# Mixture-of-experts layer of a diffusion trunk: one pass for each expert, ordered by row count, with extra rows beside the two largest and 64 rows in float32 for the smallest

## The chip, the cores and the metric

The kernel runs on one core of one Trainium2 chip. The metric is the device time of one execution in microseconds (us), as the median of repeated runs. The core has a matmul engine (TensorE, in the profile PE, and PEld for its weight loads), three engines for elementwise work (VectorE or DVE, ScalarE or ACT, GpSimd or POOL) and a queue of transfers that SyncE (SP) issues. They run side by side and wait for each other by semaphores.

## The reference

Two layers work on 384 tokens (128 of a prompt, 256 latents) of width 1024, all in float32. The change touches the last sub-layer, a mixture of eight experts of which each token takes two:

```python
D_MODEL, N_EXPERTS, TOP_K, D_FF_EXPERT = 1024, 8, 2, 1792

def swiglu(h, wg, wu, wd):
    return (jax.nn.silu(h @ wg) * (h @ wu)) @ wd

def moe_swiglu(h, w_router, wg, wu, wd):
    logits = (h @ w_router).astype(jnp.float32)
    top_v, top_i = lax.top_k(logits, TOP_K)
    top_w = jax.nn.softmax(top_v, axis=-1)
    gates = jnp.einsum('blk,blke->ble', top_w, jax.nn.one_hot(top_i, N_EXPERTS))
    y = jnp.zeros_like(h)
    for e in range(N_EXPERTS):
        y = y + gates[..., e:e + 1] * swiglu(h, wg[e], wu[e], wd[e])
    return y
```

An expert's three matrices are 1024x1792, 1024x1792 and 1792x1024 float32, 22.0 MB together. Evaluating the reference's router on its own inputs (seed 0) gives these tokens for experts 0 to 7: 60, 86, 80, 54, 96, 175, 136, 81. They sum to 768, two for each of the 384 tokens. Before this sub-layer come an even layer (convolution and pooling mixer, dense SwiGLU) and the odd layer's attention; after it a layer norm.

## The kernel before

Up to the router nothing is touched. There the kernel counts each expert's tokens on the chip and numbers them. The work of the experts is cut into **items**: an item is up to 128 rows of one expert. An expert with more than 128 rows gets a second item, and its weights are loaded a second time. The table of items (`ranks` and `items_of`, L1519 to L1536) is computed by VectorE in the middle of the first item; `more_items` gives the count of items after the first, and each engine runs one loop over them.

An item has 30 **pieces**. Each of its two halves of 896 hidden columns has eight gate/up pieces (128 input rows by 896 gate and 896 up columns, 896 KB) and seven down pieces (128 hidden rows by 1024 columns, 512 KB). SP loads each piece into one of six slots `ERAW` (L500 to L515). ScalarE casts it to fp32r, which is the high part (`expert_high`, L975), and VectorE subtracts that from the piece, which leaves the low part (`expert_low`, L1482). Both parts go to one of six slots `EWS`. The raw slot is free again when VectorE is done with it (`e_lo`), the split slot when TensorE is (`e_used`).

TensorE makes each product of the split numbers by three matmuls (`product`, L1854 to L1860): high by high, high by low, low by high. The rows of the item, 128 tokens, are the stationary side, so every matmul has 128 output rows whether they hold tokens or not. `gate_up` (L2144) has four column quarters of 448 for each piece, `down` (L2157) two halves of 512.

The loop body on TensorE is: gate/up of the first half, the down products of the second half of the item before, `turn_hidden`, gate/up of the second half, `turn_tokens` for the next item, the down products of the first half, `turn_hidden`. After the gate/up of a half, ScalarE takes the silu (`gate_silu`, L992) and VectorE the product (`hidden`, L1553). `turn_hidden` (L2171) transposes the hidden block by seven f32 transposes, and ScalarE and VectorE split it (`h_high`, `h_low`). GpSimd fetches the next item's token rows by an indirect DMA (`fetch`) and adds the weighted result into `expert_sums` in memory by another (`add_rows`). The last item is added without that detour (L2216 to L2222).

Orders on ScalarE and VectorE are written out by hand. They run about four pieces ahead of TensorE, so that `expert_highs(j, ITEM_KINDS, 4, KD + 4)` stands before `gate_silu`.

Elsewhere in the kernel, whole f32 matmuls are used: `project_out` (L1823) with 512 moving columns, the even input projection (L1760) with 384. `ada_mm` (L1720) has a stationary side of 32 columns. It writes its products for k = 0, 1, 2, 3 to the PSUM partitions from 0, 32, 64 and 96 on, which are four column groups of the array. The records show two TensorE instructions for each whole f32 matmul (L1760 stands for 128 products and has 256 records) and one for each fp32r matmul or transpose.

## Time and profile before

| | us |
|---|---|
| median of 3 runs | 1406.15 (1405.29 to 1406.32) |
| profiled execution, first to last instruction (span) | 1402.1 |
| from the start to the first matmul on expert weights | about 749.5 |
| from there to the end of the first item's products | about 59 |
| nine further items | about 557 |
| the rest of the last item, the sum, the layer norm | about 37 |

No separate whole time is listed for the profiled execution; its span is 1402.1 us and lies 4.05 us below the median. TensorE is busy 96% of the span, VectorE 62%, ScalarE 47%. A matmul's record includes the time in which it fills and drains the array, and records overlap, so the distance between starts says what a matmul costs, not its duration. The chain of waits that ended last goes 82% through TensorE and 7% through transfers.

### The profile page before, as it was taken

How to read it: one execution, taken by the hardware profiler on the slowest of the kernel's cores; microseconds unless marked ns; L12 is line 12 of the kernel's file. 1: busy time of each engine (PE TensorE's matmuls, PEld its weight loads, DVE VectorE, ACT ScalarE, POOL GpSimd, SP SyncE). 2: the span in 40 equal slices, each digit the busy share in tenths (PEclk: the TensorE clock that was granted, in tenths of full speed). 3: DMA queues.
4: the chain of work that ended last, by engine and by line, in shares of the span. 5: the costliest groups of instructions: out<-in, count | busy, mean ns of one | idle time of the engine just before them, and what ended most of it. 6: DMA issues, size and time to landing. Idle time of an engine off the chain costs nothing.

```text
span 1402.1 us, 19217 instructions
## 1 busy us (share of the span) xinstructions
PE 1348.9 (96%) x6617; PEld 1080.5 (77%) x6618; DVE 870.4 (62%) x1131; ACT 655.1 (47%) x722; POOL 114.4 (8%) x119
## 2 busy tenths in 40 slices
PE   5999999999999999999999999999999999999994
PEld 2555459999999755767478888888888888888883
DVE  1101474423424417554358787898889898898988
ACT  0101042423324322333026676777777777677772
POOL 0510005000000141000000000101010010101000
PEclk8999999999999999999988999999999999999998
DMA  9975574442433557314046899999999999999994
GB/s 366 362 304 210 208 264 147 143 155 90 158 111 105 187 186 262 123 33 165 0 181 216 291 351 354 384 382 363 373 370 383 379 376 380 358 356 384 379 341 165
DMA packets 138798, 362.60 MB, mean 259 GB/s; under 512 B 14403, under 2 KB 48422, under 8 KB 138246
## 3 DMA queue, kind: packets, MB, share of 16 engines
q1 hardware_dynamic: 132512, 339.06, 65.3%
q0 software_dynamic: 5968, 22.91, 5.2%
q8 instruction: 25, 0.41, 0.1%
q10 hardware_dynamic: 278, 0.10, 0.0%
q14 instruction: 15, 0.12, 0.0%
HBM read 351.34 MB, written 10.68 MB: 258 GB/s over the span
## 4 chain that ended last, share of the span: by engine, by line
PE 82%; DMA 7%; DVE 5%; issue 2%; ACT 2%; SPq 1%; DVEq 0%; ACTq 0%
PE ps L1858 19%; PE ps L1860 18%; PE ps L1859 18%; PE ps L1823 7%; PE ps L1760 6%; DMA sb_expert_raw<-in_moe_w_up 4%; PE ps L1950 3%; DVE sb_expert_w L1487 2%; PE ps L1720 2%; DMA sb_ring<-in_ev_w_in 2%; PE ps L2052 1%; ACT sb_expert_w L983 1%; PE ps L1694 1%; PE ps L2048 1%; PE ps L2071 1%
## 5 line engine op out<-in xcount | busy, mean ns | idle before, releaser
L1487 DVE TENSOR_TENSOR sb_expert_w<-sb_expert_raw,sb_expert_w 128x1792 fp32r<-128x1792 f32 (+1 forms) x300 | 479.6, 1648 | 45.7 <-ACT sb_expert_w L983 43.9
L983 ACT CAST sb_expert_w<-sb_expert_raw 128x1792 fp32r<-128x1792 f32 (+1 forms) x300 | 410.8, 1397 | 119.9 <-DMA sb_expert_raw<-in_moe_w_up 83.5
L1858 PE MATMUL ps<-sb_expert_w,sb_expert_x 128*128 128x448 f32 x640 | 238.7, 373 | 3.1 <-DVE sb_expert_x L1550 2.0
L1859 PE MATMUL ps<-sb_expert_w,sb_expert_x 128*128 128x448 f32 x640 | 235.6, 368 | 0.0
L1860 PE MATMUL ps<-sb_expert_w,sb_expert_x 128*128 128x448 f32 x640 | 235.5, 368 | 0.0
L1858 PEld LDWEIGHTS ps<-sb_expert_w,sb_expert_x 128*128 128x128 f32 x640 | 121.3, 189 | 15.9 <-DVE sb_expert_w L1487 3.5
L1860 PEld LDWEIGHTS ps<-sb_expert_w,sb_expert_x 128*128 128x128 f32 x640 | 121.2, 189 | 10.9
L1859 PEld LDWEIGHTS ps<-sb_expert_w,sb_expert_x 128*128 128x128 f32 x640 | 121.3, 189 | 10.0
L1858 PE MATMUL ps<-sb_split_acts,sb_split_weights 128*128 128x384 f32 x352 | 118.6, 337 | 0.4 <-issue 0.4
L1860 PE MATMUL ps<-sb_split_acts,sb_split_weights 128*128 128x384 f32 x352 | 118.6, 337 | 0.0
L1859 PE MATMUL ps<-sb_split_acts,sb_split_weights 128*128 128x384 f32 x352 | 118.3, 336 | 0.0
L1858 PE MATMUL ps<-sb_expert_w,sb_expert_h 128*128 128x512 f32 x280 | 111.7, 399 | 2.2 <-DVE sb_expert_h L1561 2.2
L1860 PE MATMUL ps<-sb_expert_w,sb_expert_h 128*128 128x512 f32 x280 | 109.8, 392 | 0.0
L1859 PE MATMUL ps<-sb_expert_w,sb_expert_h 128*128 128x512 f32 x280 | 109.8, 392 | 0.0
L1279 DVE TENSOR_TENSOR sb_scratch<-sb_scratch,ps 128x384 f32<-128x384 f32 x22 | 12.2, 555 | 143.0 <-PE ps L1860 120.6
L1270 DVE TENSOR_TENSOR sb_split_weights<-sb_ring,sb_split_weights 128x1024 fp32r<-128x1024 f32 x66 | 80.8, 1283 | 8.6 <-ACT sb_split_weights L849 8.6
L1760 PE MATMUL ps<-sb_ht,sb_ring 128*128 128x384 f32 x256 | 83.7, 487 | 1.2 <-DMA sb_ring<-in_ev_w_in 1.2
L1760 PEld LDWEIGHTS ps<-sb_ht,sb_ring 128*128 128x128 f32 x256 | 48.3, 190 | 35.9 <-issue 3.1
L778 ACT ACTIVATE sb_small<-sb_small 128x1 f32<-128x1 f32 (+1 forms) x9 | 1.8, 205 | 147.6 <-DVE sb_small L1161 127.4
L849 ACT CAST sb_split_weights<-sb_ring 128x1024 fp32r<-128x1024 f32 x66 | 65.2, 1059 | 7.2 <-PE ps L1860 7.2
L1858 PEld LDWEIGHTS ps<-sb_split_acts,sb_split_weights 128*128 128x128 f32 x352 | 66.6, 189 | 1.4 <-issue 0.5
L1859 PEld LDWEIGHTS ps<-sb_split_acts,sb_split_weights 128*128 128x128 f32 x352 | 66.6, 189 | 0.8
(296 smaller groups left out, 1811.6 us busy)
## 6 DMA issues: line engine op xcount, KB each, us to landing
sb_expert_raw<-in_moe_w_gate SPq DMA_DIRECT2D x160, 448.0 KB, 5.8
sb_expert_raw<-in_moe_w_up SPq DMA_DIRECT2D x160, 448.0 KB, 7.6
sb_expert_raw<-in_moe_w_down SPq DMA_DIRECT2D x140, 512.0 KB, 5.7
sb_ring<-in_ada_w SPq DMA_DIRECT2D x14, 3072.0 KB, 16.7
sb_ring<-in_ffn_w_gate SPq DMA_DIRECT2D x44, 256.0 KB, 3.7
sb_ring<-in_ffn_w_up SPq DMA_DIRECT2D x44, 256.0 KB, 4.6
sb_ring<-in_ffn_w_down SPq DMA_DIRECT2D x22, 512.0 KB, 6.1
sb_ring<-in_ev_w_in SPq DMA_DIRECT2D x4, 2048.0 KB, 14.8
```

Source lines behind the costliest of these rows:

```text
L849: nc.scalar.copy(WS[:, at, 0, :], RAW[:, at, :]).then_inc(hi_done, 1)
L983: nc.scalar.copy(EWS[r][:, 0, 0:w], ERAW[:, r, 0:w]).then_inc(e_hi, 1)
L1270: V.tensor_tensor(WS[:, at, 1, :], RAW[:, at, :], WS[:, at, 0, :].bitcast(F32), ALU.subtract)\
L1487: V.tensor_tensor(EWS[r][:, 1, 0:w], ERAW[:, r, 0:w], EWS[r][:, 0, 0:w].bitcast(F32), ALU.subtract)\
L1694: last = mm(PS[:, 7, 384 + 2 * k:386 + 2 * k], STG[:, n % 2, k * P:(k + 1) * P], cst("quarters"), start=True, stop=True)
L1720: last = mm(PS[q:q + 32, 6 + h, 0:384], SC[:, k, :], w[:, k, h * 384:(h + 1) * 384], start=(k < 4), stop=(k >= 4))
L1760: last = mm(PS[:, t % 4, 0:TOK], w[:, k, (t % 4) * P:(t % 4 + 1) * P], HT[:, k, :], start=(k == 0), stop=(k == KD - 1))
L1823: last = mm(PS[:, 2 * g + h, :], lhs(k)[:, g * P:(g + 1) * P], w[:, k % per, h * 512:(h + 1) * 512], start=(k == 0), stop=(k == n - 1))
L1858: first = mm(out, lh, rh, start=start, stop=False)
L1859: mm(out, lh, rl, start=False, stop=False)
L1860: return first, mm(out, ll, rh, start=False, stop=stop)
L1950: last = mm(PS[:, q, 0:480], HT[:, k, g * P:(g + 1) * P], w[:, k, :], start=(k == 0), stop=(k == KD - 1))
```

## The change

The items become **passes**, one for each expert, ranked by row count (expert 0 stays first, since it starts before the counts are known). A pass has one primary block and may have a second block of rows that uses the same loaded pieces:

```diff
+PASSES = (
+    (0, full(), None),
+    (1, full(), more_half(P)),
+    (7, half(), None),
+    (2, full(), more_quarter(P)),
+    (5, full(), None),
+    (6, full(), None),
+    (3, full(), None),
+)
```

The first number is the rank. `full` is 128 rows in split numbers as before; `half` is 64 rows, `more_half` rows 128 to 191 and `more_quarter` rows 128 to 159. Rank 4, and 128-row items for whatever rows don't fit, go through the loop, whose count is now 1 plus the left-over items. With the counts above, expert 5 (175 rows) is rank 1, expert 6 (136) rank 2, expert 3 (54) rank 7, and nothing is left over: seven passes written out and one turn of the loop, where there were ten items.

The blocks of 64 or 32 rows read the raw float32 pieces. Their stationary side has 64 (or 32) columns, and two (or four) products with different weight columns go to different column groups of the array:

```diff
+            def each_stream(outs, left, rights, start, stop):
+                made = [mm(out, left, right, start=start, stop=stop) for out, right in zip(outs, rights)]
+                return made[0], made[-1]
...
+            def gate_up_block(b, x, r, k):
+                for bank, col, lo in (*b.gate, 0), (*b.up, EW):
+                    if b.streams == 1:
...
+                    else:
+                        rights = [ERAW[:, r, lo + f * P:lo + f * P + b.width] for f in b.first]
+                        f, last = each_stream(streams(bank, b, col, b.width), x[:, cols], rights, k == 0 and col == 0,
+                                              k == KD - 1 and (b.gate[0] != b.up[0] or (bank, col) == b.up))
...
+            def down_block(b, h, col, r, start, stop):
+                if b.streams == 1:
...
+                w = D // b.streams
+                return each_stream(streams(bank, b, 0, w), h[:, cols], [ERAW[:, r, i * w:(i + 1) * w] for i in range(b.streams)],
+                                   start, stop)
```

With two streams `b.width` is 512 and `w` is 512; with four streams both are 256.

Pieces of the pass with the half block (`WHOLE`) are not split at all: `expert_high` and `expert_low` return at once. For these and for the two passes with a second block (`KEPT` = both) SP waits for TensorE before it loads into the raw slot again:

```diff
+                if piece.prior_split is None:
+                    sp.wait_ge(e_used, piece.n - (ESLOTS - 1))
+                else:
+                    sp.wait_ge(e_lo, piece.prior_split + 1)
```

The hidden block now has two buffers, and it is turned after the first 3 (full) or 5 (half) down pieces rather than after all seven:

```diff
+            def down(p, u, pieces, between, owed=True):
...
+                for j in range(spread(p)):
+                    primary(j)
+                between()
+                if more_rows:
+                    for j in range(spread(p)):
+                        secondary(j)
+                for j in range(spread(p), EB):
+                    primary(j)
+                    if more_rows:
+                        secondary(j)
...
+            def pass_products(p, before):
...
+                gate_up(p, 0, 0, False)
+                down(before, 1, [e_piece(p, KD + b) for b in range(EB)], turn_and_pick)
+                gate_up(p, KD + EB, 1, True)
+                down(p, 0, [e_piece(p, 2 * KD + EB + b) for b in range(EB)], turns)
```

`gate_up` waits for the turned hidden block before it (`hidden_split`). ScalarE's order in a pass is:

```diff
+            def pass_highs(p, before):
+                turn = KD + spread(before) + 4
+                expert_highs(p, 0, KD + 4)
+                gate_silu(p, 0)
+                expert_highs(p, KD + 4, turn)
+                h_high(p, 0)
+                expert_highs(p, turn, KD + EB + 4)
+                y_out(before)
+                expert_highs(p, KD + EB + 4, 2 * KD + EB + 4)
+                gate_silu(p, 1)
+                turn = min(ITEM_N, 2 * KD + EB + spread(p) + 4)
+                expert_highs(p, 2 * KD + EB + 4, turn)
+                h_high(p, 1)
+                x_high(p + 1 if isinstance(p, int) else (p[0], p[1] + 1))
+                expert_highs(p, turn, ITEM_N)
```

VectorE's is the same with the low parts, with `select(after)` and `picked(after)` for the next pass in it. In the first pass VectorE makes the tables. It does so now by ranks (`ranks`, `by_rank` twice, `left_over`, `passes_of` twice) where it had `ranks` and `items_of` three times:

```diff
+            expert_lows(0, 2, 4)
+            ranks()
+            by_rank(IX[:, 0:NE], "pass_of")
+            by_rank(CAP, "rows_of")
+            expert_lows(0, 4, 5)
+            left_over()
+            expert_lows(0, 5, 6)
+            dve.wait_ge(h_stored, 16 * NG)
+            passes_of(0, cand("cand_expert"))
+            expert_lows(0, 6, 7)
+            passes_of(1, FROM)
+            V.tensor_copy(TAB[:, :], TF).then_inc(tab_ready, 1)
+            more = more_items(dve)
             picked(0)
+            select(1)
+            expert_lows(0, 7, KD + 2)
             picked(1)
+            hidden(0, 0)
```

The operations of `passes_of` are over 24 x 24 = 576 elements of one partition, those of `items_of` over 16 x 16 = 256. GpSimd fetches and adds the second blocks' rows by indirect DMAs of their own.

## Rows read from the trace of the kernel before

**Rows 1.** The page, part 2: busy tenths in 40 slices of 35 us.

```profile
PE   5999999999999999999999999999999999999994
...
PEclk8999999999999999999988999999999999999998
...
GB/s 366 362 304 210 208 264 147 143 155 90 158 111 105 187 186 262 123 33 165 0 181 216 291 351 354 384 382 363 373 370 383 379 376 380 358 356 384 379 341 165
```

**Rows 2.** Stages: length, busy us (instructions) by engine; granted clock, DMA share, GB/s.

```profile
745.00:808.50 63.50, 58.51 (x281) 52.50 (x280) 54.42 (x63) 41.22 (x31) 1.23 (x2) 0.92 0.80 278
808.50:1365.00 556.50, 555.41 (x2736) 492.09 (x2735) 492.26 (x416) 413.23 (x324) 43.82 (x36) 1.00 0.99 370
1365.00:1402.10 37.10, 18.20 (x63) 11.43 (x62) 30.78 (x48) 10.91 (x16) 1.18 (x2) 0.81 0.44 173
```

**Rows 3.** The chain of waits: the hidden block's transposes at equal places of successive items.

```profile
1025.40 0.76 PE ps L2175 x7
...
1087.01 0.76 PE ps L2175 x7
```

**Rows 4.** Timeline of TensorE, gate/up: start us, duration us, what.

```profile
1057.17 0.37 PE L1859 MATMUL ps<-sb_expert_w,sb_expert_x 128*128 128x448 f32 x1
...
1057.98 0.37 PE L1860 MATMUL ps<-sb_expert_w,sb_expert_x 128*128 128x448 f32 x1
```

**Rows 5.** Timeline of TensorE, down products of the last item, six instructions apart.

```profile
1370.14 0.39 PE L1859 MATMUL ps<-sb_expert_w,sb_expert_h 128*128 128x512 f32 x1
...
1371.50 0.39 PE L1859 MATMUL ps<-sb_expert_w,sb_expert_h 128*128 128x512 f32 x1
```

**Rows 6.** Timeline of TensorE, whole f32 matmuls of the output projection.

```profile
677.34 13.90 PE L1823 MATMUL ps<-sb_ring,sb_ht 128*128 128x512 f32 x32
```

**Rows 7.** Timeline of TensorE and its weight loads, four column groups.

```profile
61.10 2.79 PE L1720 MATMUL ps<-sb_ring,sb_silu_cond 128*32 128x384 f32 x32
...
61.45 0.13 PEld L1720 LDWEIGHTS ps<-sb_ring,sb_silu_cond 128*32 128x32 f32 x4 [0.19 <-issue]
```

**Rows 8.** Timeline of TensorE, the last before and the first after them.

```profile
60.37 0.81 PE L1760 MATMUL ps<-sb_ht,sb_ring 128*128 128x384 f32 x2
...
63.82 0.91 PE L1760 MATMUL ps<-sb_ht,sb_ring 128*128 128x384 f32 x2
```

**Rows 9.** By tile, the raw pieces: duration in ns as min/median/max.

```profile
L983 ACT CAST sb_expert_w<-sb_expert_raw x300: 1041/1692/1722, 741.5 to 1370.1; 128x1792 fp32r<-128x1792 f32 x80, 128x1024 fp32r<-128x1024 f32 x70
L1487 DVE TENSOR_TENSOR sb_expert_w<-sb_expert_raw,sb_expert_w x300: 1215/2017/2028, 743.2 to 1372.8; 128x1792 fp32r<-128x1792 f32 x80, 128x1024 fp32r<-128x1024 f32 x70
...
DMA to landing us min/median/max: 3.2/6.8/12.4
```

**Rows 10.** The page, part 6: transfers, KB each, median us to landing.

```profile
sb_expert_raw<-in_moe_w_gate SPq DMA_DIRECT2D x160, 448.0 KB, 5.8
...
sb_expert_raw<-in_moe_w_down SPq DMA_DIRECT2D x140, 512.0 KB, 5.7
```

**Rows 11.** Timeline of VectorE in the first item.

```profile
757.30 0.41 DVE L1532 TENSOR_TENSOR sb_scratch<-sb_constants,sb_scratch 1x256 f32<-1x256 f32 x1
...
758.63 0.16 DVE L1536 TENSOR_TENSOR sb_scratch<-sb_scratch,sb_constants 1x16 f32<-1x16 f32 x1
...
766.47 5.88 DVE L1487 TENSOR_TENSOR sb_expert_w<-sb_expert_raw,sb_expert_w 128x1792 fp32r<-128x1792 f32 x3
...
773.56 1.09 DVE L1556 TENSOR_TENSOR sb_scratch<-sb_scratch,ps 128x896 f32<-128x896 f32 x1
```

**Rows 12.** Stages at TensorE's longest pause in the first item, as Rows 2.

```profile
771.00:774.80 3.80, 0.81 (x9) 0.73 (x7) 3.56 (x9) 3.47 (x3) 1.04 (x2) 0.88 0.94 308
774.80:780.60 5.80, 5.80 (x19) 5.33 (x20) 4.89 (x4) 2.79 (x3) 0.19 (x1) 0.50 1.00 385
```

**Rows 13.** Waits of 800 to 1350 us: total us, times, longest.

```profile
ACT sb_scratch L995 <- PE ps L1860: 34.2, 15, 3.9
```

**Rows 14.** Timeline of TensorE, the first down product of the last half.

```profile
1368.41 0.49 PE L1858 MATMUL ps<-sb_expert_w,sb_expert_h 128*128 128x512 f32 x1 [2.20 <-DVE sb_expert_h L1561]
```

More of the change, by code:

```diff
@@ L61, with __init__, home, full @@
 ESLOTS = 6
-CODES = 3 * NE
 SCRATCH = 13504
-TABLE = 16
+TABLE = 24
+CANDS = 3 * NE
+Piece = namedtuple("Piece", "n r land whole split prior_split")
+class Rows:
+    def __init__(self, streams, start, gate, up, turned, tokens, down):
+        self.streams, self.start, self.n = streams, start, P // streams
+        self.blocks = {1: EB, 2: 4, 4: 2}[streams]
+        self.first = {1: (0,), 2: (0, EB - 4), 4: (0, 2, 4, EB - 2)}[streams]
+        self.width = self.blocks * P
+        self.gate, self.up, self.turned, self.tokens, self.down = gate, up, turned, tokens, down
+    def home(self, b):
+        st = max(i for i, f in enumerate(self.first) if f <= b)
+        return (b - self.first[st]) * P + st * self.n
+def full(start=0):
+    return Rows(1, start, (0, 0), (2, 0), (0, 0), (2, 0), (4, 0))
+def half(start=0):
+    return Rows(2, start, (0, 0), (1, 0), (0, 0), (2, 0), (4, 0))
+def more_half(start):
+    return Rows(2, start, (6, 0), (7, 0), (7, 0), (7, 0), (6, 0))
+def more_quarter(start):
+    return Rows(4, start, (7, 0), (7, 256), (7, 0), (7, 0), (6, 0))
+PASSES = (
[7 more added lines that the diff above has]
+)
+NS = len(PASSES)
+LOOP_RANK = 4
+SECOND = [p for p, (_, _, sec) in enumerate(PASSES) if sec]
+WHOLE = [p for p, (_, b, _) in enumerate(PASSES) if b.streams > 1]
+KEPT = SECOND + WHOLE
+assert not {NS - 1, 0} & set(KEPT)
+SPREAD = {1: 3, 2: 5}
+def of_rank(pick):
+    return [pick(next((p for p, x in enumerate(PASSES) if x[0] == r), NS)) for r in range(NE)]
+PASS_OF = of_rank(lambda p: p)
+ROWS_OF = of_rank(lambda p: P if p == NS else sum(b.n for b in PASSES[p][1:] if b))
 def columns(parts):
@@ new lines, in h_low, with pass_lows @@
+            def h_low(p, u):
+                if p in WHOLE:
+                    return
+                b = blocks_of(p)[0]
+                dve.wait_ge(eht_hi, units_seen(p, u, 1))
+                bank = 6 if (p, u) == (0, 0) else b.turned[0]
+                V.tensor_tensor(EHS[u][1][:, 0:b.width], two(bank)[:, 0:b.width], EHS[u][0][:, 0:b.width].bitcast(F32),
+                                ALU.subtract).then_inc(eht_lo, 1)
+            def pass_lows(p, before):
+                after = p + 1 if isinstance(p, int) else (p[0], p[1] + 1)
+                turn = KD + spread(before) + 4
+                expert_lows(p, 0, 4)
+                select(after)
+                expert_lows(p, 4, KD + 4)
+                hidden(p, 0)
+                expert_lows(p, KD + 4, turn)
+                h_low(p, 0)
+                picked(after)
+                expert_lows(p, turn, 2 * KD + EB + 4)
+                hidden(p, 1)
+                turn = min(ITEM_N, 2 * KD + EB + spread(p) + 4)
+                expert_lows(p, 2 * KD + EB + 4, turn)
+                h_low(p, 1)
+                x_low(after)
+                expert_lows(p, turn, ITEM_N)
@@ L1592, in _ @@
+            for p in range(1, NS):
+                pass_lows(p, p - 1)
             per = 6
@@ L2157, in down @@
-            def down(pieces, v, second, owed):
-                pe.wait_ge(eht_lo, v + 1)
-                for b, (n, r, _) in enumerate(pieces):
-                    pe.wait_ge(e_lo, n + 1)
-                    for h in range(2):
-                        cols = slice(h * 512, (h + 1) * 512)
-                        first, last = product(PS[:, 4 + h, :], halves(EHS, slice(b * P, (b + 1) * P)),
-                                              (EWS[r][:, 0, cols], EWS[r][:, 1, cols]),
-                                              not second and b == 0, second and b == EB - 1)
-                        if owed and (b, h) == (0, 0):
-                            first.then_inc(e_used, 1)
-                    last.then_inc(yd if second and b == EB - 1 else e_used, 1)
@@ L2171, in turn_hidden, with pick, rows @@
-            def turn_hidden(v, owed):
-                pe.wait_ge(eh, v + 1)
-                for b in range(EB):
-                    last = tr(PS[:, 6 + b // 4, (b % 4) * P:(b % 4 + 1) * P],
-                              EH.rearrange("p a n -> p (a n)")[:, b * P:(b + 1) * P], ident)
-                    if owed and b == 0:
+            def pick(p):
+                more_rows = blocks_of(p)[1]
+                pe.wait_ge(mp_ready, seen(p, 1))
+                if p == 0:
+                    one = slice(0, 1)
+                else:
+                    one = bass.ds(expert_of(pe, p), 1)
+                def rows(out, hot, signal):
+                    for g in range(NG):
+                        last = mm(out, hot[:, g, :], TW[:, one, g, :].rearrange("p e c -> p (e c)"), start=(g == 0), stop=(g == NG - 1))
+                    last.then_inc(signal, 1)
+                out, out2 = pick_banks(p)
+                rows(out, PM, pick_ps)
+                if more_rows:
+                    pe.wait_ge(mp_ready, seen(p, 2))
+                    rows(out2, PM2, pick_ps)
```

746 lines of the change are left out of this document (508 added, 238 removed).

## The prediction

> **What bounds the kernel now.** I read the page's slices first: TensorE is at nine tenths or more nearly everywhere, at full clock, and the transfers move 350 to 384 GB/s in the second half [rows 1]. So the experts' stage has two candidates, and the view by stages decides. From 808.5 to 1365 us TensorE is busy 555.4 of 556.5 us, VectorE 492.3, ScalarE 413.2 [rows 2]. Nine items fit, 61.8 us each. In the chain of waits the same transposes come back after 61.6 us [rows 3]. One item's transfers are 16 x 896 KB and 14 x 512 KB [rows 10], 22.0 MB. In 61.6 us that is 357 GB/s, while up to 384 were moved with TensorE still fed (the rest is the indirect traffic of rows). TensorE is the bound, and the transfers follow about 5% behind: whatever makes TensorE much faster in one pass meets them there.
>
> TensorE's 61.6 us check from below. Starts of gate/up matmuls of 448 columns are (1057.98 - 1057.17) / 4 = 0.203 us apart [rows 4], those of down matmuls of 512 columns (1371.50 - 1370.14) / 6 = 0.227 us [rows 5]. An item has 2 x 8 x 4 x 3 = 192 of the first and 14 x 2 x 3 = 84 of the second: 38.9 + 19.1 = 58.0 us. The other 3.6 us are 22 transposes and three small matmuls.
>
> **What goes.** Ten items become seven full passes and one of 64 rows. By the reference's counts nothing is left over, and the loop turns once. Three times 61.6 us of full-width work goes: -184.8 us. VectorE's 492.3 / 9 = 54.7 us per item stays below 61.6, so a full pass stays TensorE's at 61.6.
>
> **What the narrow blocks cost on TensorE.** A whole f32 matmul is two instructions. 32 of 512 columns took 13.90 us, of which the last is 0.59: 13.31 / 31 = 0.429 us each [rows 6], 0.86 per product, one after another. What column groups do is seen in the modulation's matmuls: 32 instructions of 384 columns in four groups took 2.79 us, the last 0.49, so eight rounds of four start (2.79 - 0.49) / 7 = 0.33 us apart, and the weight loads come in fours every 0.13 + 0.19 = 0.32 us [rows 7]. One such instruction alone takes 0.429 x 384 / 512 = 0.32. Four groups ran in the time of one. Two groups of 64 columns are not in the trace. The bounds are full overlap and none; I take full overlap, by the nearest row.
>
> - 64 rows: 16 pieces with two pairs and 14 with one are 46 pairs, each two rounds of 0.429: 39.5 us. Without overlap 79.
> - 32 rows: 46 quadruples of 256 columns, 0.429 each: 19.7 us. Without overlap 79.
>
> Changing between the full width and the groups costs something each time. The last full-width instruction began at 60.37 + 0.81 - 0.49 = 60.69 and the first grouped one at 61.10, 0.09 more than the usual 0.32. The last round began at 61.10 + 7 x 0.33 = 63.40 and the next full-width one at 63.82, 0.10 more, and the second after it another 0.10 later (0.91 - 0.49 = 0.42) [rows 7, 8]. I take 0.3 us for a change and back. In a pass with a second block there are 16 in gate/up and 2 x 5 in down: 26 x 0.3 = 7.8 us. The bounds are 0 and twice that.
>
> Turning the narrow blocks and picking their rows takes 2.4, 2.5 and 2.0 us, at 0.11 us a transpose as in seven in 0.76 [rows 3]. So the pass of 64 rows is 41.9 us of TensorE, the extra 64 rows 39.5 + 2.5 + 7.8 = 49.8, the extra 32 rows 19.7 + 2.0 + 7.8 = 29.5. Net work: -184.8 + 121.2 = **-63.6 us**.
>
> The Trainium skill, "TensorE: Matmul & The Clock Gate", Measured speedup vs the span model, lists three column tiles as worth 2.38 times one, not 3. By that ratio, 0.79 a tile, the 98.7 us of grouped rounds would be 125, and the time 26 us above the forecast. This trace has four in the time of one. The page "TensorEngine Tiling (Array Packing)", Key Properties, says that a change of tiling mode drains the engine; by that rule, the trace agrees, with the 0.3 us above.
>
> **What comes back.** The new order turns the hidden block after three down pieces (3 x 6 x 0.227 = 4.1 us) instead of behind seven. ScalarE waits for the gate/up's end 34.2 us in 15 times, 2.3 each [rows 13], so it is there, and silu and product, some 0.9 and 1.1 us, end before the turn. I cost this at nothing in full passes. If that cover were gone, each half would lose up to 2 us.
>
> The raw slots are another matter. In the pass of 64 rows and the two with second blocks a slot is free only when TensorE has used the piece. A load into it lands some 6.8 us later, and if the piece is split, ScalarE needs 1.7 and VectorE 2.0 us more [rows 9]. Where narrow down pieces (0.86 us each) are followed by split pieces, six slots don't cover that chain of 10.5 us:
> - start of the third written-out pass (rank 7, 64 rows): its first down pieces reload slots that its own gate/up frees. About 2 us late.
> - start of the fourth (rank 2): its first piece waits for the second of seven down pieces 0.86 us apart. The transfers (2.4 us a gate/up piece at 384 GB/s) are behind too, then 3.7 us of splitting. TensorE is ready after some 7.5 us, the piece after 12: 4.7 us.
> - middle of the fourth: the same, and ScalarE's and VectorE's orders put the splits of two new pieces ahead of the turned hidden block (`turn` = 8 + 5 + 4), for which the gate/up waits. 7.5 us.
>
> Together 14 us, between 0 and 25. The pass of 64 rows itself needs 22.0 MB / 0.37 = 59 us of transfers against 41.9 of its own work. But the down products of the second half of rank 1, with their extra rows, lie in it, and six slots smooth the rest; I count nothing more.
>
> After a pause of 3.0 us at 771.8 the clock was 0.50 (1.2 GHz) for 5.8 us of dense work [rows 12], so about 3.4 us were lost with the rest of that fall. Two pauses of 4.7 and 7.5 us: +6.8 us.
>
> **The first pass.** VectorE makes more tables. An operation of 256 elements takes 0.41, one of 16 elements 0.16 [rows 11], so 576 take 0.74. Before: 6 + 12 operations, 6.1 us. Now: 20 small ones, about 4.0, and 6 x 0.78 = 4.7: 8.7 us. The second one-hot for rank 1 and the pick moved ahead of piece 7 add 0.8. The split of piece 7, which began at 766.5, comes 3.4 us later, and a second `picked` makes it 4.9 before the product of the hidden block, which was at 773.56 [rows 11]. TensorE waited for that product already, so the delay is on the path: +5 us (bounds 0 and 9).
>
> **The end.** The last half waited 2.2 us for the split of its hidden block [rows 14]; that is done early now. Next is the loading of the sums and VectorE's work on them, almost as late: -1 us.
>
> **Sum.** -63.6 + 14 + 6.8 + 5 - 1 = -38.8 us. The span of 1402.1 becomes 1363.3. The profile lists no other time for its execution; the median lies 4.05 above the span and I keep that: **1367 us**, range of this case 1352 to 1383.
>
> **Rivals.**
> - *The groups don't overlap.* Then a 64-row block costs 39.5 us more twice and the 32-row block 59.2 more; some 6 of it vanish in the waits. 1367 + 132 = 1499, slower. The point where it decides: of the 138 us that overlap saves, 39 must fail. Against it stand the rounds of four [rows 7]; for it only that pairs of 64 columns are not shown. 0.06.
> - *The table gives a left-over item.* If the counts on the chip were others than the reference's, for instance over 64 in the smallest, one more loop turn costs 61.6: 1429, slower. Ten items in the trace fit the counts (two above 128). 0.03.
> - *Partial overlap*, as by the ratio in the skill's sentence, worked from rows: if a round of 0.429 took 0.54, 98.7 us would be 125: 1393. 0.09.
> - *The clock falls in the pass of 64 rows.* TensorE would be idle a quarter of it. At 0.50, 39.5 us of rounds become 79, less the waits that this fills (10): 1397. For it: the clock fell at a pause of 3 us. Against: pauses there are mostly under 1 us, and grouped matmuls elsewhere ran at 1.00. 0.08.
> - *The waits don't come* (loads land in 4 us and the first pass hides its tables): -63.6 + 2 + 1 - 1: 1345. 0.12.
> - Forecast 0.62.
>
> The range to hold the time 8 in 10: 1345 to 1395. Within 0.2% (2.8 us) a measurement of this kernel can tell nothing from no change. Faster: all but the first two, 0.90; same 0.01; slower 0.09.
>
> **What would show it.** In the changed kernel's profile: 30 pieces x 8 loads of expert weights, not 10 items' worth. L2175's successor comes back after 61.6 us in full passes, about 111 in rank 1's. Grouped matmuls of 512 columns start in pairs at about 0.43 us. TensorE pauses of over 3 us stand only at the start and in the middle of the fourth pass, with the clock at 0.50 behind them, and one of about 5 us longer in the first. VectorE and ScalarE are nearly empty in the pass of 64 rows. The prediction is wrong if pairs start 0.86 us apart, or if the full passes come out longer than 62 us.

## The result, and the profile after

The changed kernel takes 1382.93 us (median of 4 runs, 1380.95 to 1385.3), the kernel before beside it 1406.06. The ratio is 0.9847, with an interval of 0.9824 to 0.987. The forecast was 1367 in a range of 1345 to 1395: the direction and the range held, and of the 39 us forecast 23 came. The profiled execution took 1383.09 us with a span of 1381.2, so 1.9 us lie around the span. If as much lay around the span of before, that profile (1402.1) was of an execution some 2 us quicker than the median. So the two profiles differ by 20.9 us where the medians differ by 23.1; the forecast, which kept the distance of 4.05 us between span and median, is to be held against the medians.

The page's slices of the changed kernel (tenths of busy time and of the granted clock, 40 slices of 34.5 us), against [rows 1]:

```profile
PE   5999999999999999999999799999789999999994
...
PEclk8999999999999999999996899999998999999997
```

TensorE's row dips at three slices: the 23rd (from 760 us, the first pass) and the 29th and 30th (966 to 1036 us, the 64-row pass and the one behind it). The clock's row has a new 8 right behind them.

The stages (length, busy us and instructions by engine, granted clock, DMA share, GB/s), against [rows 2]: the first pass, everything from there to the last down products, the end; then, out of the second, the later part of the 64-row pass (its second gate/up and five down pieces), what follows up to the middle of rank 2's pass, the second part of rank 2's pass, and two full passes.

```profile
752.80:820.35 67.55, 59.23 (x277) 52.74 (x277) 54.95 (x78) 37.24 (x30) 2.38 (x4) 0.90 0.76 260
820.35:1345.60 525.25, 500.39 (x2609) 365.22 (x2609) 338.38 (x291) 286.04 (x236) 48.63 (x34) 0.98 0.83 305
1345.60:1381.20 35.60, 17.03 (x55) 10.48 (x53) 29.48 (x47) 8.58 (x14) 1.19 (x2) 0.80 0.42 158
958.24:985.86 27.62, 23.93 (x110) 7.84 (x109) 0.69 (x1) 3.39 (x5) 4.65 (x6) 0.94 1.04 378
985.86:1039.00 53.14, 40.62 (x277) 26.06 (x276) 25.35 (x24) 23.10 (x18) 0.00 (x0) 0.91 0.76 278
1039.00:1088.30 49.30, 47.19 (x340) 33.00 (x340) 25.85 (x18) 20.34 (x20) 7.08 (x4) 0.96 0.63 207
1222.01:1345.60 123.59, 123.59 (x609) 109.69 (x608) 110.01 (x92) 92.29 (x75) 18.37 (x8) 1.00 0.99 373
```

Read the second line first. Before, TensorE was idle 1.1 us of 556.5. Now it is idle 24.9 of 525.3, and VectorE has fallen from 88% to 64% of the stretch. The two full passes at the bottom show no TensorE idle time at all, at 61.8 us each, so what is lost lies in the passes with narrow blocks. The timeline of TensorE gives the places (start, duration, what, idle time just before and what ended it):

```profile
777.11 0.74 PE L2526 MATMUL ps<-sb_expert_w,sb_expert_x 128*128 128x448 f32 x1 [5.44 <-DVE sb_expert_w L1755]
785.23 1.75 PE L2652 MATMUL ps<-sb_constants,sb_scratch 128*128 128x128 f32 x7 [2.84 <-DVE sb_scratch L1900]
869.51 0.44 PE L2526 MATMUL ps<-sb_expert_w,sb_expert_x 128*128 128x448 f32 x1 [1.24 <-DVE sb_expert_w L1755]
939.58 0.47 PE L2526 MATMUL ps<-sb_expert_w,sb_expert_h 128*128 128x512 f32 x1 [0.94 <-DVE sb_expert_w L1755]
970.41 7.07 PE L2532 MATMUL ps<-sb_expert_raw,sb_whole_x 128*64 128x512 f32 x24 [2.27 <-DMA sb_expert_raw<-in_moe_w_up]
980.25 1.08 PE L2532 MATMUL ps<-sb_expert_raw,sb_whole_h 128*64 128x512 f32 x4 [1.03 <-DMA sb_expert_raw<-in_moe_w_down]
991.51 0.54 PE L2526 MATMUL ps<-sb_expert_w,sb_expert_x 128*128 128x448 f32 x1 [3.71 <-DVE sb_expert_w L1755]
1039.01 0.71 PE L2526 MATMUL ps<-sb_expert_w,sb_expert_x 128*128 128x448 f32 x1 [8.82 <-DVE sb_static_rows L1778]
1088.28 0.45 PE L2526 MATMUL ps<-sb_expert_w,sb_expert_x 128*128 128x448 f32 x1 [2.10 <-DVE sb_expert_w L1755]
1125.52 0.44 PE L2526 MATMUL ps<-sb_expert_w,sb_expert_x 128*128 128x448 f32 x1 [1.05 <-DVE sb_expert_w L1755]
1146.13 0.47 PE L2526 MATMUL ps<-sb_expert_w,sb_expert_x 128*128 128x448 f32 x1 [1.88 <-DVE sb_expert_w L1755]
```

The rows at 939.58, 991.51 and 1039.01 are the three forecast pauses. Those at 869 (rank 1's pass), at 970 and 980 (inside the 64-row pass) and at 1088, 1125 and 1146 (rank 5's pass, the fifth) were not forecast. Inside the 64-row pass the releaser is a DMA, not a split: the queue moved 378 GB/s at a DMA share of 1.04, so there the transfers' own rate looks like the limit (run 6 tests it).

From stage to stage, by the two profiles (a pass ends here where the next one's first expert matmul starts):

| stretch | before | after | difference | forecast |
|---|---|---|---|---|
| start to first expert matmul | 749.7 | 752.8 | +3.1 | 0 |
| first pass | 59.5 | 67.5 | +8.0 | +5 |
| further passes, to the last down products | 556.8 | 525.2 | -31.6 | -42.8 |
| end | 36.1 | 35.6 | -0.5 | -1 |

The first line is not the change's: the code there is the same, and repeats of one kernel differ by more (the last section). Experiments are therefore compared by their medians and, in the profile, by the **middle stretch**: from the first expert matmul to the last turning of a hidden block (1338.50 in the changed kernel). It leaves out the time before the experts and the end, which both scatter. It is 1338.50 - 752.83 = 585.7 us in the changed kernel and 586.0 in a second profile of it. The kernel before turns its last hidden block at another place, so its stretch isn't comparable, and run 1 stands for it. Each stretch is read from one profiled execution; only the changed kernel has two. Single pauses scatter more than the stretch does: the one at 869.51 (1.24 us) is under 0.5 us in the second profile, and the last one in rank 5's pass is 1.03 there for 1.88.

### The profile page after: what moved, and what is told of

Its sections match the earlier page's. It is cut to its first block, busy times and chain, and to the rows that moved or that the text cites. A ratio compares the mean times of both kernels' runs of the same rounds, so it can differ in the third digit from the quotient of the medians.

```text
span 1381.2 us, 17263 instructions
## 1 busy us (share of the span) xinstructions
PE 1300.3 (94%) x6503; PEld 959.1 (69%) x6504; DVE 718.9 (52%) x1021; ACT 525.1 (38%) x632; POOL 120.5 (9%) x119
## 4 chain that ended last, share of the span: by engine, by line
PE 82%; DMA 7%; DVE 6%; SPq 2%; ACT 2%; issue 1%; DVEq 0%; ACTq 0%
PE ps L2526 9%; PE ps L2528 8%; PE ps L2527 8%; PE ps L2224 8%; PE ps L2226 8%; PE ps L2225 8%; PE ps L2189 7%; PE ps L2126 6%; PE ps L2532 5%; DMA sb_expert_raw<-in_moe_w_up 4%; PE ps L2316 3%; DVE sb_expert_w L1755 2%; DMA sb_ring<-in_ev_w_in 2%; PE ps L2086 2%; PE ps L2418 1%
## 5 line engine op out<-in xcount | busy, mean ns | idle before, releaser
L1755 DVE TENSOR_TENSOR sb_expert_w<-sb_expert_raw,sb_expert_w 128x1792 fp32r<-128x1792 f32 (+1 forms) x210 | 339.0, 1648 | 130.4 <-ACT sb_expert_w L1204 129.6
L1204 ACT CAST sb_expert_w<-sb_expert_raw 128x1792 fp32r<-128x1792 f32 (+1 forms) x210 | 287.1, 1392 | 178.9 <-DMA sb_expert_raw<-in_moe_w_down 88.4
L2526 PE MATMUL ps<-sb_expert_w,sb_expert_x 128*128 128x448 f32 x448 | 171.9, 384 | 27.5 <-DVE sb_expert_w L1755 16.7
L2527 PE MATMUL ps<-sb_expert_w,sb_expert_x 128*128 128x448 f32 x448 | 166.9, 373 | 0.0
L2528 PE MATMUL ps<-sb_expert_w,sb_expert_x 128*128 128x448 f32 x448 | 166.8, 372 | 0.0
L2526 PEld LDWEIGHTS ps<-sb_expert_w,sb_expert_x 128*128 128x128 f32 x448 | 86.5, 193 | 57.6 <-issue 34.2
L2528 PEld LDWEIGHTS ps<-sb_expert_w,sb_expert_x 128*128 128x128 f32 x448 | 86.3, 193 | 7.7
L2527 PEld LDWEIGHTS ps<-sb_expert_w,sb_expert_x 128*128 128x128 f32 x448 | 86.6, 193 | 7.1
L2526 PE MATMUL ps<-sb_expert_w,sb_expert_h 128*128 128x512 f32 x196 | 79.9, 408 | 0.9 <-DVE sb_expert_w L1755 0.9
L2528 PE MATMUL ps<-sb_expert_w,sb_expert_h 128*128 128x512 f32 x196 | 77.4, 395 | 0.0
L2527 PE MATMUL ps<-sb_expert_w,sb_expert_h 128*128 128x512 f32 x196 | 77.1, 393 | 0.0
L2224 PEld LDWEIGHTS ps<-sb_split_acts,sb_split_weights 128*128 128x128 f32 x352 | 66.5, 189 | 1.3 <-issue 0.5
L2225 PEld LDWEIGHTS ps<-sb_split_acts,sb_split_weights 128*128 128x128 f32 x352 | 66.6, 189 | 0.9
L2226 PEld LDWEIGHTS ps<-sb_split_acts,sb_split_weights 128*128 128x128 f32 x352 | 66.6, 189 | 0.0
```

What stands on the lines that cost most here:

```text
L1204: nc.scalar.copy(EWS[r][:, 0, 0:w], ERAW[:, r, 0:w]).then_inc(e_hi, 1)
L1755: V.tensor_tensor(EWS[r][:, 1, 0:w], ERAW[:, r, 0:w], EWS[r][:, 0, 0:w].bitcast(F32), ALU.subtract)\
L2224: first = mm(out, lh, rh, start=start, stop=False)
L2225: mm(out, lh, rl, start=False, stop=False)
L2226: return first, mm(out, ll, rh, start=False, stop=stop)
L2526: first = mm(out, lh, rh, start=start, stop=False)
```

## Experiments

**1. Neither narrow block.** The new code with all ten blocks at full width; the rows over 128 go to the loop.

```diff
-    (1, full(), more_half(P)),
-    (7, half(), None),
-    (2, full(), more_quarter(P)),
+    (1, full(), None),
+    (7, full(), None),
+    (2, full(), None),
```

> All passes full and split, no second blocks, rank 7 full: only the new order, the ranks' tables and the early turn of the hidden block are left of the change, with ten passes again. Theory A (narrow work as forecast, losses in slots that TensorE holds, beside the pass of 64 rows): the first pass's tables cost 8 us as in the changed kernel, the rest nothing: 1414. Rival B (the new order itself costs in every pass): 9 passes at 1 to 2 us more, 1425 or above. Rival C (the transfers' own rate is what stopped TensorE in the changed kernel): 1414 too.

Measured: 1412.29 us (10 runs, 1406.28 to 1414.73), ratio 1.0034 (1.0013 to 1.0055). The middle stretch is 616.1 us. The first pass is 66.5 us for 59.5 before, and after it the expert passes show no TensorE pause over 0.3 us. So the new order of turning the hidden block costs nothing in full passes, and the first pass, with its new tables and picks, costs 7.0 us more. That is what theories A and C had (1414); rival B (1425 or above) is out.

**2. Second blocks alone.** Rank 7 stays full.

```diff
-    (7, half(), None),
+    (7, full(), None),
```

> Second blocks kept (64 rows beside rank 1, 32 beside rank 2), rank 7 full and split. TensorE's work is 61.6 - 41.9 = 19.7 us more than in the changed kernel. Theory A: nearly all of the some 30 us of pauses go with the pass of 64 rows: 1383 + 20 - 27 = 1376, faster than the changed kernel. Rival B: pauses stay as they are: 1403. Rival C: with TensorE the bound in every pass the pauses go too, 1376, but then only one pass with little work can be at fault, and the run with rank 7 alone must show 22.0 MB / 0.37 = 59 us or more for it.

Measured: 1382.72 us (4 runs, 1378.86 to 1387.09), ratio 0.9843 (0.9802 to 0.9884). The middle stretch is 585.8 us. Both are those of the whole change. Theories A and C both said 1376, rival B 1403, and none came: with rank 7 full there are still idle times of 9.7 us before TensorE's matmuls from the first pass's end to the last turn, the longest 1.9 us each at 983.03, 1088.63 and 1126.12.

**3. The 64-row pass alone.** Ranks 1 and 2 have no second block.

```diff
-    (1, full(), more_half(P)),
+    (1, full(), None),
     (7, half(), None),
-    (2, full(), more_quarter(P)),
+    (2, full(), None),
```

> Rank 7 as 64 rows in whole float32, no second blocks; nine and a half full passes. Theory A: against the run with neither, -19.7 us of work, and the late splits behind it come back (start and middle of the pass after, 4.7 and 9 us, the clock's fall 3 to 5): 1414 - 20 + 18 = 1412. Rival B: 1425 - 20 = 1405. Rival C: the pass is held at 59 us by the transfers' rate, so it saves 2 to 3 us, with TensorE pausing inside the pass and not in the next: 1411.

Measured: 1419.01 us (8 runs, 1409.61 to 1420.5), ratio 1.0087 (1.0063 to 1.0111). The middle stretch is 623.7 us, 7.6 more than in run 1. All three expectations (1405 to 1412) were too low. The time inside its 64-row pass, one pause in it, and the one in the middle of the pass behind it:

```profile
905.30:936.00 30.70, 25.57 (x116) 9.23 (x116) 3.07 (x9) 3.69 (x5) 2.96 (x4) 1.00 1.02 384
```

```profile
917.83 1.94 PE L2532 MATMUL ps<-sb_expert_raw,sb_whole_x 128*64 128x512 f32 x8 [2.46 <-DMA sb_expert_raw<-in_moe_w_up]
...
979.31 0.71 PE L2526 MATMUL ps<-sb_expert_w,sb_expert_x 128*128 128x448 f32 x1 [9.29 <-DVE sb_static_rows L1778]
```

The idle times inside the 64-row pass and the down products in it sum to 5.9 us, where the queue moves 384 GB/s at a share of 1.02. The two pauses in the pass behind it, at its start (4.21 us) and in its middle (9.29), sum to 13.5. So the transfers' rate and the late splits both take their part, the splits the larger. Between full passes, which leave the transfers hardly any slack (373 GB/s at a share of 0.99 above), the 64-row pass is a loss. Runs 1 to 3 and the change make a table of two by two, against run 1:

| | TensorE's work by the forecast's durations | median | middle stretch | so lost |
|---|---|---|---|---|
| second blocks alone | -2 x 61.6 + 49.8 + 29.5 = -43.9 | -29.6 | -30.3 | 14 |
| 64-row pass alone | 41.9 - 61.6 = -19.7 | +6.7 | +7.6 | 27 |
| both | -63.6 | -29.4 | -30.4 | 33 |

On top of the second blocks the 64-row pass is worth nothing: 0.1 us of the middle stretch, and nothing in the medians, which are uncertain by some 3. The three kernels ran on one chip; for the changed one's first runs none is named. Its repeat, on another chip, beside run 9 gave nearly the same middle stretch (586.0).

**4. The order around the turned hidden block.** In rank 2's pass ScalarE and VectorE do the hidden block's work before the splits of the next two pieces. The same edit stands in both engines' orders.

```diff
-                turn = KD + spread(before) + 4
+                turn = KD + EB if before in WHOLE else KD + spread(before) + 4
```

> The changed kernel, but ScalarE and VectorE turn to the hidden block of the pass after the 64-row pass before they split that pass's next pieces (turn at 15 instead of 17). Theory A: of the pause of 9.4 us in the middle of the fourth pass some 3.5 are this order; the rest is the load and the split of the piece. 1379, and a pause of 6 us. Rival: the piece is last anyhow, pause 9.4 and 1383 as before.

Measured: 1377.65 us (4 runs, 1372.27 to 1382.94), ratio 0.9817 (0.9768 to 0.9865). The middle stretch is 583.1 us, 2.6 less. The pause in the middle of rank 2's pass:

```profile
1030.17 0.71 PE L2526 MATMUL ps<-sb_expert_w,sb_expert_x 128*128 128x448 f32 x1 [4.38 <-DVE sb_expert_w L1755]
```

It fell from 8.82 to 4.38 us, and its releaser is now the split of the piece itself. About half of that pause was the order, and the rest is the late piece, as theory A had it. The middle stretch shows only 2.6 of the 4.4 us, since other pauses of this profile are longer (1.76 for 0.94 us at the third written-out pass, 2.67 for 2.27 inside the 64-row pass). They stand ahead of any edited code, so they are scatter between executions and no effect of the edit.

For runs 4 to 7 the interval of the ratio overlaps that of the changed kernel (0.9824 to 0.987), and they ran on two other chips than its repeat. So the medians alone don't settle what one edit is worth; the places in the profile do, and in part the middle stretch.

**5. Second products of rank 2 right behind the first.** In `down`, for the block of 32 rows only:

```diff
+                early = more_rows and more_rows.streams == 4
                 for j in range(spread(p)):
                     primary(j)
+                    if early:
+                        secondary(j)
                 between()
-                if more_rows:
+                if more_rows and not early:
```

> The changed kernel; where the second block is 32 rows (rank 2), each of the first down pieces has its second block's products at once, before the hidden block is turned, so that its raw slot is free some 3 to 5 us earlier. Theory A (late release of slots that TensorE holds): the pauses at the start and in the middle of the fifth pass (2.5 + 0.9 and 1.4 + 3.6 us in the changed kernel's profile) go, 1383 - 6 = 1377. Rival C (the transfers' own rate): the pauses stay, 1383, since the same bytes are to come.

Measured: 1380.42 us (4 runs, 1370.55 to 1384.36), ratio 0.979 (0.9745 to 0.9835). The middle stretch is 583.9 us, 1.8 less. By the starts of TensorE's matmuls rank 5's pass lost 7.4 us before and loses 1.4 now. The pauses ahead of it are longer in this profile (at the third written-out pass 2.2 for 1.3, at rank 2's start 4.8 for 4.1, in its middle 9.7 for 9.2), and the clock at rank 2's start was 0.50 for 6.8 us instead of 3.4, together 3.7 us. The edited code runs only after them, so this is scatter between executions too; it hides most of the 6.0 us in the middle stretch. The one pause left in rank 5's pass:

```profile
1146.55 0.47 PE L2526 MATMUL ps<-sb_expert_w,sb_expert_x 128*128 128x448 f32 x1 [1.25 <-DVE sb_expert_w L1755]
```

**6. Lighter transfers in the 64-row pass.** Of rank 7's up weights 128 of 896 columns are loaded; its up products read what the slot held. The piece shrinks from 896 to 512 KB.

```diff
+                w = P if piece.whole else EW
+                cols = slice(u * EW, u * EW + w)
-                sp.dma_start(ERAW[:, r, EW:2 * EW], moe_w_up[0, one, rows, cols]...
+                sp.dma_start(ERAW[:, r, EW:EW + w], moe_w_up[0, one, rows, cols]...
```

> The changed kernel, but in the pass of 64 rows only 128 of the 896 up columns of each gate/up piece are loaded (16 x 0.39 MB less; the rest of the slot holds what was there), so this leaves a part of rank 7's weights out. Same instructions, waits and slots. Rival C (the transfers' rate holds the pass): the pauses inside its second gate/up (6.5 us) go and the next pass begins without its 4.3 us: with the clock some 13 us less, 1370. Theory A (slots only): landing takes 4 us instead of 7 to 9.6, the chains of release, load and split stay: 5 us less at most, 1378; the pause of 9.4 us in the middle of the fourth pass stays in both, since its chain begins after the light loads.

Measured: 1377.18 us (4 runs, 1374.7 to 1380.76), ratio 0.9799 (0.9773 to 0.9825). The middle stretch is 582.4 us, 3.3 less. Inside the pass the longest pause left is 0.58 us, and the two pauses of rank 2's pass do not shrink (4.90 for 3.71 us, 8.79 for 8.82):

```profile
982.79 0.71 PE L2528 MATMUL ps<-sb_expert_w,sb_expert_x 128*128 128x448 f32 x1 [4.90 <-DVE sb_expert_w L1757]
...
1031.48 0.71 PE L2528 MATMUL ps<-sb_expert_w,sb_expert_x 128*128 128x448 f32 x1 [8.79 <-DVE sb_static_rows L1780]
```

So two things were at work. The rate of the transfers makes the pauses inside the 64-row pass: there rival C was right. Those of rank 2's pass come from the chain behind a slot that comes free late (load, cast, subtraction), which lighter loads ahead of it didn't shorten: there theory A was right, and the total is nearer to its 1378 than to C's 1370.

**7. The first pass in another order.** VectorE splits piece 7 before the tables of `passes_of(1)`, and `picked(1)` comes behind `hidden(0, 0)`.

```diff
-            expert_lows(0, 6, 7)
+            expert_lows(0, 6, 8)
             passes_of(1, FROM)
...
-            expert_lows(0, 7, KD + 2)
-            picked(1)
+            expert_lows(0, 8, KD + 2)
             hidden(0, 0)
+            picked(1)
```

> The changed kernel; VectorE splits piece 7 before the second table and the picks, and picks for rank 1 after the product of the hidden block. Theory (tables stand before what TensorE waits for): of the two pauses of 5.8 and 3.1 us in the first pass some 5 us go, and one of the clock's falls: 1383 - 6 = 1377. Rival (another wait takes their place, or the clock falls anyway): 1381 to 1383.

Measured: 1378.87 us (4 runs, 1377.39 to 1382.69), ratio 0.9811 (0.9784 to 0.9838). The middle stretch is 582.1 us, 3.6 less, and the first pass 64.0 for 67.5. The two pauses of the first pass:

```profile
777.50 2.71 PE L2498 MATMUL ps<-sb_scratch,sb_temp 128*128 x12 [3.28 <-DVE sb_temp L1861]
...
782.10 1.76 PE L2652 MATMUL ps<-sb_constants,sb_scratch 128*128 128x128 f32 x7 [1.89 <-DVE sb_scratch L1900]
```

Idle before them is 5.17 us where it was 8.28: the 3.1 us are nearly the whole gain. Around them the clock was at 0.50 for 10.2 us, as long as in the changed kernel, so the fall that was expected to go stayed.

**8. No overlap between column groups.** Every product of a narrow block is written to, and summed in, the first column group. Work, order and loads stay; the results of the other groups are left out.

```diff
-                made = [mm(out, left, right, start=start, stop=stop) for out, right in zip(outs, rights)]
+                made = [mm(outs[0], left, right, start=start and right is rights[0], stop=stop and right is rights[-1])
+                        for right in rights]
```

> The changed kernel with all two or four products of each_stream written to the first column group, summed there (so the narrow blocks' results are left wrong). Same instructions, loads and waits, no overlap. If column groups are what makes the narrow blocks cheap, a pair takes 1.72 us instead of 0.86 and a quadruple 1.72 instead of 0.43: +39.5 +39.5 +59.2 us of rounds, less some 25 us of pauses that this fills in the 64-row pass and behind it: 1383 + 113 = 1496. If the groups gave nothing, no change: 1383.

Measured: 1493.79 us (one run), for the 1496 expected. One piece's products of 64 rows and the first matmul behind them, and one piece's products of 32 rows, in this kernel and then in the changed one:

```profile
822.83 3.65 PE L2532 MATMUL ps<-sb_expert_raw,sb_second_x 128*64 128x512 f32 x8
826.41 0.47 PE L2526 MATMUL ps<-sb_expert_w,sb_expert_x 128*128 128x448 f32 x1
...
1054.82 3.64 PE L2532 MATMUL ps<-sb_expert_raw,sb_second_x 128*32 128x256 f32 x16
```

```profile
829.32 0.47 PE L2526 MATMUL ps<-sb_expert_w,sb_expert_x 128*128 128x448 f32 x1
...
831.95 1.94 PE L2532 MATMUL ps<-sb_expert_raw,sb_second_x 128*64 128x512 f32 x8
833.82 0.47 PE L2526 MATMUL ps<-sb_expert_w,sb_expert_x 128*128 128x448 f32 x1
...
995.67 1.07 PE L2532 MATMUL ps<-sb_expert_raw,sb_second_x 128*32 128x256 f32 x16
```

Eight instructions of 64 by 512 columns take 3.65 us in one group and 1.94 in two; sixteen of 32 by 256 take 3.64 in one group and 1.07 in four. The overlap saves 110.7 us of span; without it the change is 86 us slower than the kernel before (1407.87 beside it).

**9. The better versions.** The first takes edit 2 (no 64-row pass) with edits 5 and 7, and was run twice on different chips. The second takes the changed kernel with edits 4, 5 and 7. The changed kernel itself ran again beside the second.

> Second blocks, no 64-row pass, with the early second products of rank 2 and the moved tables: if pauses and tables add up, 1383 - 6 - 6 = 1371; if the pass of 64 rows was worth something after all that the tables hid, 1377 or more.

> The version with second blocks, early second products and moved tables, without the 64-row pass, again beside the others on one chip: 1373, 618 us from the first expert matmul on.

> The changed kernel with all three edits: turn at 15, rank 2's second products early, the tables moved. If they add: 628.4 us from the first expert matmul to the end, less 4.7, less 5, less 5.7: 613, that is 1383 - 15 = 1368. Beside the version without the 64-row pass (1373): the pass is then worth some 5 us. Rival: the pauses of the 64-row pass and behind it take it back: 1373.

> The changed kernel itself, on the chip and in the rounds of the others: 1383, 628 us from the first expert matmul on. What its runs differ by (1381 to 1385 so far) stands before the experts, where the clock falls in some runs for 10 us and in others for 20.

| | us, runs | ratio | middle stretch |
|---|---|---|---|
| second blocks, 5 and 7 | 1373.41 (4) | 0.9774 (0.9747 to 0.98) | 575.0 |
| the same again | 1372.35 (5) | 0.9754 (0.9731 to 0.9776) | none |
| both, 4, 5 and 7 | 1372.33 (5) | 0.9752 (0.973 to 0.9775) | 575.7 |
| changed kernel again | 1383.87 (5) | 0.9836 (0.981 to 0.9862) | 586.0 |

One further execution of the repeat took 6352.44 us, the one that was profiled; median and ratio leave it out, and the last section tells what its trace shows. Both versions beat both kernels: the one before by 32 to 36 us, the changed one by 11.5 us in the medians on one chip and by 10 to 11 in the middle stretch. Without the 64-row pass edits 5 and 7 take 10.8 us off run 2's middle stretch (585.8 to 575.0), and of the two pauses of 1.80 and 1.89 us in rank 5's pass 0.24 us is left. Between the two versions there is no difference: 0.7 us of middle stretch, and 0.0 us of median on one chip, 1.1 across chips. So the rival expectation of 1373 came and not the 1368, and even with three edits around it the 64-row pass brings nothing that can be measured. Its two pauses in the last version:

```profile
984.11 0.71 PE L2526 MATMUL ps<-sb_expert_w,sb_expert_x 128*128 128x448 f32 x1 [4.71 <-DVE sb_expert_w L1755]
...
1027.56 0.71 PE L2526 MATMUL ps<-sb_expert_w,sb_expert_x 128*128 128x448 f32 x1 [4.78 <-DVE sb_expert_w L1755]
```

## Why the prediction was right in direction and 16 us short

**Removed and added work: held.** The profile's page counts 128 gate transfers of weights, 16 for each of eight passes. A gate/up piece with its second block comes back after 833.82 - 829.32 = 4.50 us; the forecast's parts are 12 x 0.203 + 4 x 0.429 + 0.3 = 4.45. Full passes take 61.8 us against the 61.6 of [rows 3]. One sign read otherwise: the transposes of rank 1's second half come 97.5 us after those of the pass before, not 111, since a part of its second block's products lies behind them, partly in rank 7's pass.

**Overlap: held.** [rows 7] showed only four groups of 32; two groups of 64 overlap just as fully (run 8). Had the Trainium skill's ratio of 2.38 for three column tiles ("TensorE: Matmul & The Clock Gate", Measured speedup vs the span model) ruled here, a pair could not have run in 0.43 us: carried over at 0.79 a tile it makes 0.54, an estimate from that page. The page's row is for three tiles of 32 columns, so this case shows only that it does not carry over to pairs of 64; the measurement decides. The 0.3 us for a change of the engine's tiling and back held too: the piece above takes 4.50 us, and its matmuls alone make 4.15.

**The three forecast pauses: held in sum.** Counted from start to start, less the usual distance, they are 1.3, 4.1 and 9.2 us, 14.6 for 14. The chain of waits shows the whole way to the start of rank 2's pass (start, duration):

```profile
980.12 0.34 SPq L685
980.55 7.05 DMA sb_expert_raw<-in_moe_w_up
987.62 1.69 ACT sb_expert_w L1204
989.34 2.04 DVE sb_expert_w L1755
991.51 0.54 PE ps L2526
```

Load 7.05, cast 1.69, subtraction 2.04: with the gaps 11.4 us from the issue to the matmul, for the 10.5 worked out from [rows 9]. In the middle of the pass TensorE's releaser is `sb_static_rows`, VectorE's pick for the next pass. The chain there is a load of 7.09 us, cast and subtraction, then the subtraction for the turned hidden block (1.00) and the picks, which VectorE has in this order. Behind the pause at rank 2's start the clock was at 0.50 for 3.4 us and behind the one in its middle for 3.9, so some 3.7 us were lost where 6.8 were counted.

**The 64-row pass itself, for which the prediction says "I count nothing more": failed.** By starts 6.1 us are lost inside it, 1.7 of them by a fall of the clock. The prediction had both numbers, 59 us of transfers against 41.9 of work, and covered the difference with "six slots smooth the rest". Six slots hold at most 6 x 0.92 = 5.5 MB, some 15 us of transfers at 378 GB/s, and TensorE's waits for split pieces at 939.58 and 991.51 suggest that they held nothing ready early in the pass and at its end; how full they were was not measured. Run 6 shows the rate as the cause of these pauses, run 3 what the pass costs without a slower pass beside it. The rival with a clock fall in this pass named the place, but its price of 30 us did not come. The clock fell for one stretch of 3.4 us, behind the pause of 2.27 us:

```profile
971.23:974.64 3.41, 3.41 (x10) 0.86 (x8) 0.00 (x0) 0.00 (x0) 1.78 (x2) 0.50 1.03 419
```

**The fifth pass: left out.** The prediction worked the slot chain out for the pass behind rank 1's and the one behind rank 7's, and not for the one behind rank 2's second block, where it holds as well. Three down pieces are held until their second products come, behind the turn. It cost 7.4 us by starts. A pause in rank 1's pass cost 1.4 more; no run isolates it. The chain to one of the pauses in rank 5's pass:

```profile
1076.12 0.61 PE ps L2532 x8
...
1079.39 8.30 DMA sb_expert_raw<-in_moe_w_up
1087.71 1.70 ACT sb_expert_w L1204
1089.43 2.04 DVE sb_expert_w L1755
```

Run 5 moved the second products ahead, and of these pauses only the one of 1.25 us was left.

**The first pass: +8.0 for +5.** The tables delay the split of piece 7 as forecast. The prediction treated a later product of the hidden block as the only way this reaches TensorE. TensorE waited 5.44 us for piece 7 first, then 2.84 for the hidden block, where it had waited 2.99 for the block alone before. That is 5.3 us more, and around these waits the clock was at 0.50 for 10.2 us instead of 6.8, which costs 1 to 1.7 us more. Run 1 has 7.0 of the 8.0 us with the same tables and no narrow block, and run 7 gives 3.5 of them back by order alone.

**The end: -0.5 for -1.** The wait of [rows 14] is gone, and what is late next is the sums, as forecast. Before the last 12 products TensorE now waits longer than before (kernel before, then after; 2.72 in the changed kernel's second profile):

```profile
1380.77 7.08 PE L2220 MATMUL ps<-sb_scratch 128*128 128x512 f32 x12 [2.46 <-DVE sb_scratch L1635]
```

```profile
1359.92 7.08 PE L2712 MATMUL ps<-sb_scratch 128*128 128x512 f32 x12 [4.37 <-DVE sb_scratch L2001]
```

**The sum of the further passes:** -63.6 + 14.6 + 3.7 + 6.1 + 7.4 + 1.4 = -30.4, measured -31.6; 1.2 us stay unexplained. So the terms that the prediction had (work, three pauses, two clock falls) stand within some 3 us together, and its miss is what it put at nothing: 6.1 and 8.8 us in these passes, and 3 us of the first pass. The pauses came to 29.5 us, over the bound of 25 that the prediction set for them. That 1382.93 still lies within its narrow range (1352 to 1383) owes something to luck: the clock falls cost 3.1 us less than forecast. The wide range (1345 to 1395) held without it. More slots, and the early second products of run 5 for the block of 64 rows too, were not tried.

## What to carry to other kernels

When a pass does less arithmetic on the same bytes, first divide its bytes by the rate that the trace shows at a full queue. What lies above the engine's time is lost unless slower passes beside it have slack and there are slots to carry it over (that more slots would have done it here is argued and not shown). Here 19.7 us of saved matmuls brought nothing, while rows added beside loaded weights paid. Where a slot's release moves from an early reader to a late one, work the reload chain (landing, cast, subtraction) out for every border between passes, not only for the ones where the code looks new. And test parts of a change alone: the 64-row pass alone made the kernel slower, and the total hid it.

## What was not expected of the hardware

The time before the experts differs between executions of the same code by more than several of the effects here. From 735 to 745 us, first in the changed kernel's profile, then in its repeat:

```profile
735.00:745.00 10.00, 9.75 (x47) 9.17 (x46) 3.16 (x10) 4.95 (x9) 0.57 (x1) 0.50 0.34 136
```

```profile
735.00:745.00 10.00, 7.46 (x66) 7.06 (x65) 7.55 (x16) 9.32 (x9) 0.57 (x1) 1.00 0.45 159
```

The granted clock is 0.50 in the one and 1.00 in the other. The program there, transposes and small products, is the same. The first expert matmul is at 752.8 us and at 745.5. The two executions took 1383.09 and 1374.22 us, so 7.3 of the 8.9 us between them were made before the experts' first matmul.

The loads that TensorE ended up waiting for took 7 to 9.6 us to land with the queue full (960.76 to 970.37 is the longest of those in the 64-row pass), against the median of 6.8 in [rows 9]; a chain worked out with the median is up to 3 us short just where it matters.

The execution of 6352.44 us was slow on TensorE alone. Here is one group of fp32r matmuls, first in the profile of the same kernel at 1372.22 us, then in this one:

```profile
L2527 PE MATMUL ps<-sb_expert_w,sb_expert_x 128*128 128x448 f32 x512 | 188.7, 368 | 0.0
```

```profile
L2527 PE MATMUL ps<-sb_expert_w,sb_expert_x 128*128 128x448 f32 x512 | 566.0, 1105 | 0.0
```

A matmul's record is 1105 ns long for 368, and TensorE is busy 100% of the span. VectorE's subtractions take 1651 ns for 1649 and ScalarE's casts 1387 for 1393, and the loads land sooner (4.2 us for 7.3 in the median of the up weights). The page of this execution has no row of the granted clock. Why TensorE was slow stays open.
